# A two-layer sequence model on one core: the norm's root moved from the input of the products to their results, and two chains reordered

## What is computed

```python
# layer 1 (width 1024, 512 positions)
u = rmsnorm(h, g_mix);  z = u @ w_in           # 61 column tiles of 128
y_gla  = gated linear attention (4 heads) ; y_conv = cb * conv(cc * cx) ; y_swa = windowed attention
h = h + (sum of sigmoid(gates_i) * (y_i @ w_i)) @ w_o
u = rmsnorm(h, g_ffn);  h = h + (silu(conv(u @ w_up)[:F]) * conv(u @ w_up)[F:]) @ w_down
h = rmsnorm(h, g_final)
# layer 2 (16 meta tokens in front: 528 positions)
proj = rmsnorm_2(h, norm1_w) @ w_in_2
out_a = hgrn2_mixer(q, f_pre, i_in, g)          # 8 heads: log, cumulative sum, exp, chunked scan
out_b = mamba2_mixer(z, xbc, dt_pre)            # conv of 4 taps, silu, 16 heads in pairs, 2 groups of B and C
h = h + concat(out_a, out_b) @ w_out
h = h + conv_glu_ffn(rmsnorm_2(h, norm2_w), ...);  y = rmsnorm_2(h, final_norm_w)

def rmsnorm(x, g): return x * rsqrt(mean(x * x) + EPS) * g
```

## Time and profile before

| | us |
|---|---|
| median of 3 runs (1867.45 to 1870.22) | 1869.77 |
| profiled execution, its own time | 1866.25 |
| its span in the profile | 1864.5 |
| TensorE busy (share of the span) | 1784.2 (96%) |
| VectorE busy | 1062.8 (57%) |
| ScalarE busy | 749.2 (40%) |

### The profile page before, as it was taken

How to read it: one execution, slowest core, us unless ns; L and a number is a source line. 1 busy time by engine, 2 the same in 40 slices (tenths; PEclk the granted TensorE clock), 3 DMA queues, 4 the chain that set the end, 5 groups by cost and what they waited for, 6 DMA issues and landing times.

```text
span 1864.5 us, 27001 instructions
## 1 busy us (share of the span) xinstructions
PE 1784.2 (96%) x11004; PEld 1540.9 (83%) x11004; DVE 1062.8 (57%) x1635; ACT 749.2 (40%) x1130; POOL 8.2 (0%) x10
## 2 busy tenths in 40 slices
PE   5999999999989999999799999989998799999997
PEld 2877777778868888888598989889988699999885
DVE  5455545555466666633556465766787666666323
ACT  4444434332243333322446565544454433333221
POOL 0000000000000000000000000000000000000000
PEclk9999999999999999999899999999999899999999
DMA  4222222222322333333122212122212132332331
GB/s 167 79 79 80 79 90 69 90 80 92 101 68 90 94 99 98 95 94 98 46 80 64 73 58 80 57 69 69 69 61 66 56 91 91 91 93 93 99 101 57
DMA packets 44331, 154.21 MB, mean 83 GB/s; under 512 B 5793, under 2 KB 6049, under 8 KB 44209
## 3 DMA queue, kind: packets, MB, share of 16 engines
q1 hardware_dynamic: 44208, 152.50, 26.6%
HBM read 150.39 MB, written 2.10 MB: 82 GB/s over the span
## 4 chain that ended last, share of the span: by engine, by line
PE 90%; DVE 6%; ACT 2%; issue 1%; SPq 0%; DMA 0%; ACTq 0%; DVEq 0%
PE ps L555 88%; PE ps L559 2%; DVE full L1384 1%; DVE u_lo L1214 1%; ACT arena L848 1%; DVE arena L1217 1%; DVE arena L1224 1%; DVE h_res L1214 0%; ACT r_bc L848 0%; DMA w_raw<-weights 0%; ACT full L848 0%; DVE w_lo L1214 0%; DVE r_bc L1214 0%; DVE h_res L1384 0%; ACT w_hi L848 0%
## 5 line engine op out<-in xcount | busy, mean ns | idle before, releaser
L555 PE MATMUL ps<-u_hi,w_hi 128*128 128x264 f32 (+3 forms) x2376 | 652.4, 328 | 33.1 <-DVE u_lo L1214 30.6
L555 PE MATMUL ps<-u_hi,w_lo 128*128 128x264 f32 (+3 forms) x2376 | 643.3, 324 | 0.0
L555 PE MATMUL ps<-u_lo,w_hi 128*128 128x264 f32 (+3 forms) x2376 | 641.7, 323 | 0.0
L1214 DVE TENSOR_TENSOR w_lo<-w_raw,w_hi 128x1024 fp32r<-128x1024 f32 x280 | 343.0, 1225 | 257.1 <-ACT w_hi L848 241.1
L555 PEld LDWEIGHTS ps<-u_hi,w_hi 128*128 128x128 f32 (+1 forms) x2376 | 396.7, 189 | 88.4 <-issue 34.3
L555 PEld LDWEIGHTS ps<-u_lo,w_hi 128*128 128x128 f32 (+1 forms) x2376 | 396.5, 189 | 36.5 <-issue 1.1
L555 PEld LDWEIGHTS ps<-u_hi,w_lo 128*128 128x128 f32 (+1 forms) x2376 | 397.1, 189 | 35.3 <-issue 1.0
L848 ACT ACTIVATE w_hi<-w_raw 128x1024 fp32r<-128x1024 f32 x280 | 297.0, 1061 | 209.2 <-PE ps L555 174.5
L1224 DVE SCALAR_TENSOR_TENSOR ffn<-ps,par,ffn 128x512 f32<-128x512 f32 (+2 forms) x176 | 132.0, 750 | 163.4 <-ACT ffn L848 160.2
L848 ACT ACTIVATE arena<-ps 128x512 f32<-128x512 f32 (+7 forms) x218 | 97.2, 485 | 239.2 <-PE ps L555 148.3
L848 ACT ACTIVATE ffn<-ps,par 128x512 f32<-128x512 f32 x88 | 64.6, 734 | 296.9 <-PE ps L555 296.9
(11 more groups left out here) (132 smaller groups left out, 1418.2 us busy)
## 6 DMA issues: line engine op xcount, KB each, us to landing
w_raw<-weights SPq DMA_DIRECT2D x280, 512.0 KB, 3.6
h_res<-xT SPq DMA_DIRECT2D x4, 512.0 KB, 5.1
outT<-h_res SPq DMA_DIRECT2D x8, 256.0 KB, 2.1
cst<-consts SPq DMA_DIRECT2D x1, 730.0 KB, 8.5
seg<-consts SPq DMA_DIRECT2D x1, 256.0 KB, 8.7
par<-params SPq DMA_DIRECT2D x1, 243.5 KB, 6.5
msk<-cmask SPq DMA_DIRECT2D x1, 128.0 KB, 8.9
h_res<-metaT SPq DMA_DIRECT2D x1, 64.0 KB, 8.2
```

The source lines that it names most:

```text
L555: return nc.tensor.matmul(out, lhsT, rhs, start=start, stop=stop)
L1214: return V.tensor_tensor(out, a, b, op)
```

## The change

- **Root at the evacuation.** The product now runs on h_res x gain (step `raw`: ScalarE makes u_hi, VectorE u_lo, as each h_res k is ready), and every group that reads u is multiplied by the root r_bc by VectorE as it leaves PSUM. What ScalarE took out of PSUM before it now takes from SBUF, after VectorE. TensorE's product with ones moves into the first or second group after the residual (SUMS_AT). For up and up2 the conv taps run from a copy in SBUF, one group later (`finish_up`). norm1's double root is made from one weighted sum.
- **Start.** The parameters and two of the eight input tiles are loaded first, then the first slab, then the other input; the constants go behind the third slab.
- **HGRN2.** Ln and scan of `prep` after hq (`prep_ln`), Exp after hi (`prep_exp`), the rest after hg.
- **State-space stage.** mb 1 and mc 1 move into the loop, `ssm_bc` 1 to after oh 4; mz comes earlier than mx at the start; each conv is in two parts (`conv1`, `conv2`), the second after the next group; its first tap moves from ScalarE to VectorE; `ssm_gate` comes right after `ssm_c`.
- **Slots.** The first group of layer 2 takes the slot that lies on only one of layer 1's slots. At the end of the output product, `raw` and `square` of tile k stand one group later.

The diff, its core:

```diff
 
 
-SSM_ORDER = [("mx", 0), ("mz", 0), ("oh", 0)]
-for _t in range(M2_T):
-    SSM_ORDER += [("mz", _t)] if _t else []
-    SSM_ORDER += [("mx", _t + 1)] if _t + 1 < M2_T else []
-    SSM_ORDER += {0: [("oh", 1), ("oh", 2)], 1: [("oh", 3), ("oh", 4)], 2: [("oh", 5), ("oh", 6)], 3: [("oh", 7)],
-                  4: [("om", (0, 0)), ("om", (0, 1))], 5: [("om", (0, 2)), ("om", (0, 3))], 6: [("om", (0, 4))],
-                  7: [("om", (0, 5)), ("om", (0, 6)), ("om", (0, 7))]}[_t]
-SSM_ORDER += [("om", (1, m)) for m in range(KD)]
+SSM_ORDER = [("mz", 0), ("mz", 1), ("mx", 0), ("oh", 0), ("mx", 1), ("mb", 1), ("oh", 1), ("oh", 2), ("mx", 2),
+             ("mc", 1), ("oh", 3), ("mx", 3), ("mz", 2), ("oh", 4), ("oh", 5), ("mx", 4), ("mz", 3), ("oh", 6),
+             ("oh", 7), ("mx", 5), ("mz", 4), ("om", (0, 0)), ("om", (0, 1)), ("mx", 6), ("mz", 5), ("om", (0, 2)),
+             ("om", (0, 3)), ("mx", 7), ("mz", 6), ("om", (0, 4)), ("mz", 7), ("om", (0, 5)), ("om", (0, 6)),
+             ("om", (0, 7))] + [("om", (1, m)) for m in range(KD)]
+
+
+SSM_PIECES = {("mz", 0): ["dt 0"], ("mx", 0): ["zero 0"], ("oh", 0): ["bc 0"], ("mx", 1): ["a 0"], ("mb", 1): ["b 0"],
+              ("oh", 1): ["c 0"], ("oh", 2): ["a 1"], ("mx", 2): ["b 1"], ("mc", 1): ["c 1"], ("oh", 3): ["a 2"],
+              ("mx", 3): ["b 2"], ("mz", 2): ["c 2"], ("oh", 4): ["bc 1"], ("oh", 5): ["a 3"], ("mx", 4): ["b 3"],
+              ("mz", 3): ["c 3"], ("oh", 7): ["a 4"], ("mx", 5): ["b 4", "v2 0", "v2 1"],
+              ("mz", 4): ["c 4", "sum 0", "v2 2", "v2 3"], ("om", (0, 0)): ["v2 4"], ("om", (0, 1)): ["a 5"],
+              ("mx", 6): ["b 5"], ("mz", 5): ["c 5"], ("om", (0, 2)): ["v2 5"], ("om", (0, 3)): ["a 6"],
+              ("mx", 7): ["b 6"], ("mz", 6): ["c 6"], ("om", (0, 4)): ["a 7"], ("mz", 7): ["b 7"],
+              ("om", (0, 5)): ["v2 6"], ("om", (0, 6)): ["c 7"], ("om", (1, 0)): ["sum 1"]}
+CONVS = [("mb", 0), ("mc", 0)] + [x for x in SSM_ORDER if x[0] in ("mx", "mb", "mc")]
+CONV_NO = {x: n + 1 for n, x in enumerate(CONVS)}
...
-    return g % SLOTS1 if g < FIRST2 else SLOTS1 + (g - FIRST2) % SLOTS2
+    return g % SLOTS1 if g < FIRST2 else SLOTS1 + (g - FIRST2 + 1) % SLOTS2
...
-LAST1 = [max(n for n in range(FIRST2) if slot_of(n) == s) for s in range(SLOTS1)]
+LAST1 = {FIRST2 + 1: [max(n for n in range(FIRST2) if slot_of(n) == s) for s in (0, 1)],
+         FIRST2: [max(n for n in range(FIRST2) if slot_of(n) == 2)]}
...
+TAIL = ((("dt", 0), "head_d", 1), (("mb", 0), "head_a", 0), (("mc", 0), "head_b", 0), (("mz", 0), "head_c", 0),
+        (("mz", 1), "head_d", 0))
...
     for h in range(HG_H):
-        at = [(k, h + 1) for k in names] if h + 1 < HG_H else tail
-        put(names[3], h, ("prep", GLA_H + h))
-        nxt = [(k, h + 2) for k in names] if h + 2 < HG_H else tail if h + 2 == HG_H else (("mc", 1),)
-        for stage, where in zip("abcd", list(at[1:4]) + [nxt[0]]):
-            put(*where, ("head_" + stage, GLA_H + h))
-
+        n = GLA_H + h
+        if h > 1:
+            put("hf", h, ("head_d", n - 2))
+        put("hq", h, ("prep_ln", n))
+        put("hi", h, ("prep_exp", n))
+        if h:
+            put("hq", h, ("head_a", n - 1))
+            put("hi", h, ("head_b", n - 1))
+            put("hg", h, ("head_c", n - 1))
+        put("hg", h, ("prep", n))
...
         for k in range(KD):
-            put(kind, at[k], ("square", (which, k)))
+            where = at[min(k + 1, KD - 1)] if kind == "om" else at[k]
+            if which != "final":
+                put(kind, where, ("raw", (which, k)))
+            put(kind, where, ("square", (which, k)))
+        if which == "norm1":
+            put(kind, at[-1], ("bounds", 0))
         put(kind, at[-1], ("norm", which))
...
+    put("up", (2, 0), ("raw_meta", 0))
+    put("hf", 0, ("second_start", 4))
+    for part, where in enumerate((("hq", 0), ("hi", 0), ("hf", 1), ("hq", 1))):
+        put(*where, ("second_start", part))
...
+            if stage == "c":
+                pieces.append(("ssm_gate", int(n)))
+                if int(n) == M2_T - 1:
+                    pieces.append(("ssm_v2", int(n)))
+                pieces.append(("ssm_sq", int(n)))
+        at[0:0] = [("conv2", before)] if before else []
+        if where[0] == "om":
+            at[0 if not before else 1:0 if not before else 1] = pieces
+        else:
+            at.extend(pieces)
+        before = where if where in CONV_NO else None
+        at.extend([("conv1", where)] if before else [])
+    steps = [("raw", ("g_mix", 0)), ("raw", ("g_mix", 1)), ("slab", 0)]
+    steps += [("raw", ("g_mix", k)) for k in range(2, KD)] + [("slab", 1)]
+    steps += [("square", ("g_mix", k)) for k in range(KD)]
     for g in range(NG):
+        if GROUPS[g][:2] == ("gk", 0):
+            steps.append(("norm", "g_mix"))
         steps.append(("group", g))
         steps.extend(after[g])
...
+SUMS_AT = {GROUP_OF[("gk", 0)]: ("g_mix", 0), GROUP_OF[("up", (0, 0))]: ("g_ffn", 5),
+           GROUP_OF[("hf", 0)]: ("norm1", 6), GROUP_OF[("up2", (0, 1))]: ("norm2", 0)}
+ROOT_AT = {0: "g_mix", GROUP_OF[("up", (0, 0))]: "g_ffn", GROUP_OF[("hf", 0)]: "norm1",
+           GROUP_OF[("up2", (0, 0))]: "norm2"}
...
-            for k in range(0, KD, 2):
-                sp.dma_start(h_res[:, k:k + 2, META:T2], x_v[:, k:k + 2, :]).then_inc(x_in[k // 2], 16)
             sp.dma_start(par[:, :], params).then_inc(par_in, 16)
+            sp.dma_start(h_res[:, 0:2, META:T2], x_v[:, 0:2, :]).then_inc(x_in[0], 16)
...
                 if s == 0:
-                    sp.dma_start(cst[:, :], consts[:, 0:CW]).then_inc(par_in, 16)
-                    sp.dma_start(seg64, consts[:, CW:CW + SEQ]).then_inc(par_in, 16)
-                    sp.dma_start(msk[:, :], cmask).then_inc(par_in, 16)
+                    for k in range(2, KD, 2):
+                        sp.dma_start(h_res[:, k:k + 2, META:T2], x_v[:, k:k + 2, :]).then_inc(x_in[k // 2], 16)
+                if s == 2:
+                    sp.dma_start(cst[:, :], consts[:, 0:CW]).then_inc(cst_in, 16)
...
+                if g == FIRST2:
+                    pe.wait_ge(meta_lo_ok, 1)
...
+                    if g in SUMS_AT and SUMS_AT[g][1] == n:
+                        norm(SUMS_AT[g][0])
...
                 if which == "norm1":
                     pe.wait_ge(meta_sum, 1)
                     mm(ps[:, 5, 0:META], ones[:, :], ffn[:, 4, 0:META])
-                    pe.wait_ge(sq2_added, KD - 1)
-                    last = mm(ps[:, 6, :], ones[:, :], ffn[:, 0, :])
+                    mm(ps[:, 6, :], ones[:, :], r_bc[:, 0:SEQ])
+                    pe.wait_ge(scaled_sum, 1)
+                    mm(ps[:, 7, :], ones[:, :], ffn[:, 0, :]).then_inc(sum_ok, 1)
+                    return
...
+            def conv1(which):
+                act.wait_ge(ssm_sem["conv"], CONV_NO[which])
+                f(cv[1], cv[0], ACT.Tanh).then_inc(silu_ok, 1)
...
+            def raw(which_k):
+                which, k = which_k
+                if (which, k) == ("g_mix", 0):
+                    exp_ln()
+                    act.wait_ge(par_in, 16)
+                if (which, k) == ("norm1", 0):
+                    act.wait_ge(gain1_ok, 1)
+                residual_ready(act, which, k)
+                c0, c1 = norm_columns(which)
+                f(u_hi[:, k, c0:c1], h_res[:, k, c0:c1], ACT.Identity, scale=gain_of(which, k)).then_inc(u_hi_ok, 1)
...
+            def prep_ln(n):
+                exp_ln()
+                act.wait_ge(f_ok, n - GLA_H + 1)
+                f(lf2, f2[n % 2], ACT.Ln).then_inc(sp_ok, 1)
+
+            def prep_exp(n):
+                exp_ln()
+                act.wait_ge(cum_ok, n + 1)
+                act.wait_ge(ready, n)
+                f(e2[:, 0, :], bc2, ACT.Exp)
+                f(e2[:, 1, :], bc2, ACT.Exp, scale=-1.0)
+                f(h_mid, h_mid, ACT.Exp).then_inc(exp_ok, 1)
 
...
+            def finish_up():
+
+                if pending[0] is None:
+                    return
+                g = pending[0]
+                pending[0] = None
...
+                dve.wait_ge(act_part, PART_NO[g])
+                if kind == "up":
+                    link(madd(dst[:, 1:], x[:, 0:SEQ - 1], pc("fconv", 3 * c + 1), dst[:, 1:]))
+                    last = madd(dst[:, 2:], x[:, 0:SEQ - 2], pc("fconv", 3 * c), dst[:, 2:])
+                else:
+                    o = META - USED
+                    link(madd(dst, x[:, o - 1:o - 1 + SEQ], pc("fconv2", 3 * c + 1), dst))
+                    last = madd(dst, x[:, o - 2:o - 2 + SEQ], pc("fconv2", 3 * c), dst)
+                if not half:
+                    last.then_inc(up_ok, 1)
+                    return
+                link(last)
+                dve.wait_ge(silu_ok, j + 1 + (0 if kind == "up" else FT + M2_T + 2 * M2_G))
+                link(mul(ffn[:, 6, :], ffn[:, 4 + j % 2, :], dst))
+                parts(a_hi[:, j, :], a_lo[:, j, :], ffn[:, 6, :])
+
             def group(g):
...
```

(45 more changed lines are left out.)

436 lines of the change are left out of this document (187 added, 249 removed).

## The result

The changed kernel takes 1893.45 us (median of 1878.60 to 1894.00, three of its four runs at 1893 to 1894), the kernel before 1868.94. The ratio is 1.0119, 95% interval 1.0099 to 1.0139. It is slower by 1.2%, where 3.5% faster was forecast. The profiled execution has a span of 1891.9 us.

The account below looks back on a forecast made before the run. TensorE, busy 96% of the span, was taken to set the time through idle and low-clock stretches. Gains 14.9 + 10.5 + 16.0 + 15.5 + 8.5 = 65.4 from 1866.25 give 1800.8, plus 2 about 1803 us; range 1788 to 1822.

Parts of the forecast that it names:

- Start: Kernel start: the first group, ga, ends at 16.7 instead of 32.6 us; gain 14.9 us, bounds 11 and 17.
- g_ffn: Boundary after the last wo: up (0, 1) starts at 528.8 instead of 539.3 us; gain 10.5 us.
- norm1: Boundary before HGRN2: TensorE goes on at 909.7 against 925.93 us; gain 16.0 us.
- norm2: Output product and norm2: om (1, 1) to up2 (0, 1) takes 29.8 instead of 45.4 us; gain 15.5 us.
- The up and up2 stages: Stages without waits: VectorE's added work stays hidden, 9.0 of 11.1 us per pair in up, 8.7 of 11.6 in up2.
- rival 4: Slower: in up and up2, tap, slab and silu in VectorE's evacuation ring cost 75 us; kernel at 1906 us; chance 0.03.
- GLA and HGRN2 30 of 47 and 22 + 3 of 32. I take nothing for it.: GLA and HGRN2 stages: VectorE's work stays under TensorE's, so the added evacuation operations are hidden and cost 0 us.
- The chain in three places "gives 0 to 1": HGRN2: taking Ln and Exp earlier gives 0 to 1 us and is only a cover for the added operations.
- State-space stage: State-space stage: of 20.2 us to win, some 12 stay as waits and half clock; gain 8.5, bounds 17 and -5.
- the 20 that it had named as a sign of being wrong: State-space stage: over 20 us of waits there would show the prediction wrong.
- I walk its queue: State-space stage: VectorE's operations followed in order, giving waits of TensorE of 8.5 us together, 3.1 of them at om (0, 0).
- Rival 1: VectorE sets the state-space and output stages: the first gains nothing or loses 5, the second gains 12; 1816 us; chance 0.22.

Follow-up runs that it names:

- the mended one: Changed kernel with ScalarE's root of head_d before hf's tanh: one place 1840.4 us; three places, with further ScalarE steps and v2 2, 3 moved earlier, 1814.4 us.
- the last version: Changed kernel with ScalarE steps TensorE needs moved ahead of waits for VectorE, Ln and Exp behind head steps, v2 2, 3 earlier: 1805.15 us, ratio to before 0.9666.

## Why the prediction was wrong

- **Start, g_ffn, norm1, norm2: right.** 14.9, 10.5, 16.0 and 15.5 were forecast; 15.4 (16.1 less the 0.7 of the sum behind gq), 10.6, 16.6 and 14.4 came. The first product starts at 9.3 (forecast 8.9). No boundary waits for r_bc; the one wait of 2.3 is the final norm's and is there before too. Walking each boundary by its chain was the right method. Two of its sums are slightly off: the terms written give 16.2 at norm1, not 16.0, and 29.6 behind om (1, 1), not 29.8.
- **The up and up2 stages: right.** 346.9 both times, no wait in the rings; rival 4's mechanism, the ring of tap, slab and silu, did not show. Its direction came true by another ring, in the stages that it left out.
- **The step that failed: "GLA and HGRN2 30 of 47 and 22 + 3 of 32. I take nothing for it."** It took VectorE's room, work per group under TensorE's, for cover. The room was there, and more than it said (VectorE is busy 18.5 of a head's 31.9 us before, not 22, and 52% of the time after). But the root at the evacuation doesn't only add 0.7 us of work: it puts VectorE ahead of ScalarE's tanh, which used to read PSUM itself. Both queues run in order, so all that stood behind that tanh was tied to VectorE's queue, here the root that frees head_a's bank, which had been ready only 1.5 us before TensorE wanted it. That cost 42.6 us (282.4 against 239.8), and moving that root alone gives 41.8 of it back (240.6).
- **The chain in three places "gives 0 to 1":** right in the kernel before (it cost 0.8, about nothing) and in the mended one (240.1 with three, 240.6 with one), wrong in the change as made: 15.6. The prediction asked only what Ln and Exp gain by being earlier, not what stands behind them: head_a and head_b of the previous head, in both queues.
- **State-space stage: 8.5 forecast, -20.0 measured,** under the bound of -5, and with 31.1 us of waits, over the 20 that it had named as a sign of being wrong. The step that failed was "I walk its queue": one queue, VectorE's. It even names the 1.7 us in which VectorE idles for w_hi, but for pairs 5 to 7 only and not behind the convolution's tanh, nor ScalarE's v_hi behind square, table and sum's root (3.1 forecast at om (0, 0), 10.2 measured). With ScalarE's queue mended the stage gains 7.1. That is near the forecast 8.5, but for a kernel in which v2 2 and 3 and a root were moved as well, so it doesn't confirm the walk; it shows that the loss lay in ScalarE's queue and not in VectorE's work. (By its own terms the forecast is 20.2 - 11.5 = 8.7, or 8.2 with the rounded 12.)
- **Left out: gq 0 to wo 7,** -5.6. 0.7 is the moved sum. Six waits of about 0.5 before `swa_c`, 3.2 us together, are most of the rest, and go with the copy of swa_b ahead of its gate's tanh (3.6 us back in the last version). The remaining 1.3 has no cause on record.
- **Rival 1,** VectorE sets the state-space stage: not borne out down to 262.3 us. Whether it does below that wasn't tried. In the last version VectorE is busy 148 of 179 us in the middle of the stage:

```profile
1191.00:1370.00 179.00, 172.14 (x1472) 164.04 (x1470) 148.07 (x288) 81.92 (x197) 8.88 (x5) 0.97 0.23 69
```

The last version stands at 1805, near the forecast 1803, because the forecast was one for a kernel whose queues don't block each other, and because that version has moves that nobody priced in it. That is no credit to it: the diff fixed the order of ScalarE's queue, and it could be read there.

What stays open: the single run of the changed kernel at 1878.6, 15 us below the other three, has no cause on record (its mean clock, 0.981 against 0.979, makes an estimated 4 of them); why the three places cost 15.6 us on top of the root, in terms of Ln ahead of head_a, Exp ahead of head_b and the slab's place, was not measured; nor was what the first tap on VectorE costs in the state-space stage.
